# Experts' weights rotate through three places instead of two, and TensorE's expert loop runs over six experts

## The chip, the cores and the metric

The kernel runs on 1 core of one Trainium2 chip. The metric is device time in microseconds (us) from the start to the end of one launch; the median of three runs is compared. All data are float32.

## The reference

One layer of a decoder over 1024 tokens of width 1024. Three token mixers (RWKV-7, chunkwise mLSTM, sliding-window attention) are computed from one input projection, gated, merged and projected; then comes a mixture of experts, which is the part that the change touches:

```python
x = x + gt1 * hybrid_mixer(h, ...)
h = rms_norm(x, norm2_g) * (1 + sc2) + sh2
x = x + gt2 * hier_moe(h, w_rg, b_rg, w_re, b_re, w_e_in, w_e_out)

def expert_block(args):                      # 32 experts, each token goes to 2 of them
    xs, e = args                             # w_e_in[e] is 1024 x 1024, w_e_out[e] 512 x 1024
    gate, up = jnp.split(xs @ w_e_in[e], 2, axis=-1)
    return (jax.nn.silu(gate) * up) @ w_e_out[e]
```

## The kernel before

A router gives every token two of the 32 experts, and an indirect DMA sorts the tokens' rows into slots of 96 per expert (`x_slots` in DRAM). Then the 32 experts run one after the other, each with one block of up to 96 tokens. (Experts with more tokens get extra blocks behind the loop; with these inputs there are none, and that code is jumped over.)

One expert is 144 matmuls of the program on TensorE (PE). `first(s, w, j)` is one half of the product with `w_e_in` (48 matmuls for j = 0, 48 for j = 1), `second(w)` is the product with `w_e_out` (48). `step(e, ...)` waits for the weights and calls both halves of `first`; `close(e, ...)` waits for the weights of the output product and for the activations, and calls `second`. PE runs step(e), close(e - 1), step(e + 1), close(e), so that the activation of one expert (ScalarE: SiLU; VectorE: product, transposes) lies beside the next expert's first product. Each float32 matmul of the program is two LDWEIGHTS and two MATMULs in the trace: 288 MATMULs per expert.

An expert's weights are three pieces of 2048 KB: two halves of `w_e_in`, then `w_e_out`. A place in SBUF holds the three pieces of one expert. `WE` has two such places, at columns 0 and 12288 of the arena. A third set of tiles, `WX` at columns 24576 to 36863, holds expert 2 only, and is not filled again. Expert 3 goes to place 0, expert 4 to place 1, and from there on the two alternate: `next_in(e, s, used)` on SyncE (SP) waits until PE has used each half of the expert that was in place s and then issues the DMA of that half (line 468), `next_out` does this for `w_e_out` (line 472) after a wait on `y`, which counts two for each finished `second`. All of these go through SP's one DMA queue (q1) in the order written. The token rows of the experts are loaded (line 1700) and the results stored (lines 1731, 1732) through ScalarE's queue (q10).

PE's code for experts 0 to 3 is written out; experts 4 to 31 run in a loop over two experts (`pe.Fori(2, NE // 2)`, line 1351, 14 rounds). SP, ScalarE and VectorE have loops over two experts as well. In three gaps of its loop VectorE does the rest of the router's work (`blocks_counted`, `blocks_placed`, `blocks_owned`).

Behind the experts GpSimd gathers for every token its two results from `y_slots` (line 759), VectorE adds them to the rows `f_x` that SP has loaded from `x1` (line 540), and ScalarE stores the output. At the end of PE's loop, line 1360 is the branch that jumps over the code for extra blocks.

Of the kernel before, what the change touches and what calls it, by code (L numbers as in the profile page):

```python
# [5 lines left out]
T, D = 1024, 1024  # L6
P = 128
NT, KT = T // P, D // P
H, N = 4, 64
CH = 8  # L10
NG, NE, TOPK, DE = 4, 32, 2, 512
# [10 lines left out]
def hybrid_block(nc, I, out, dram):  # L22
# [6 lines left out]
    with ctx:  # L29
        SB = ctx.enter_context(nc.sbuf_tensor("arena", [P, 52992], f32))[:, :]  # L30
        PS = [ctx.enter_context(nc.psum_tensor(f"bank{i}", [P, 512], f32))[:, :] for i in range(8)]
        sems = {}

        def sem(name):
            if name not in sems:
                sems[name] = ctx.enter_context(nc.semaphore(name))
            return sems[name]

        def view(off, *dims):

            n = 1
            for d in dims:
                n *= d
            v = SB[:, off:off + n]
            if len(dims) == 2:
                v = v.rearrange("p (a b) -> p a b", a=dims[0])
            if len(dims) == 3:
                v = v.rearrange("p (a b c) -> p a b c", a=dims[0], b=dims[1])
            return v
# [7 lines left out]
        VECS, MOD1, WR_SHIFT, WR_SCALE, WR_BIAS = range(1, 6)  # L57
        COUNTS, EXTRAS, X_TABLE = range(NT + 1, NT + 4)
        IDENT, CONSTS, Q_TILE, _, _, _, R_IOTA, R_IOTAP = range(1, 9)
        COND, ADA_ROW, _, _, _, A_TANH, A_GSIG = range(1, 8)  # L60

        K_ACT, K_DVE = (1, 4, 7), (0, 2, 3, 5, 6)
# [113 lines left out]
        FW = view(0, 8, P)  # L176
        FWS = [FW, view(1024, 8, P)]
        s_fill = [sem("fill_w"), sem("fill_wb")]
        FWC = view(1024, 4, P)
        FWB, FBB = view(1536, 8, P), view(2560, 2, P)  # L180
# [97 lines left out]
        i_ix = [sb_i[:, 152:153], sb_i[:, 153:154], sb_i[:, 154:155]]  # L278

        WE = [[view(12288 * s + 4096 * j, 4, 1024) for j in range(3)] for s in range(2)]  # L280
        WX = [view(32768, 4, 1024), view(24576, 4, 1024), view(28672, 4, 1024)]
        e_xs = [view(TMP0 + 2322 + D * s, D) for s in range(2)]
        e_xT = [view(TMP0 + KT * CAP * s, KT, CAP) for s in range(2)]
        e_h, e_hT, e_g = view(36864, 3, P), view(37248, 4, CAP), view(37632, 3, P)
        e_hTl = view(38784, 4, CAP)
# [1 line left out]
        E_GU = [PS[3], PS[4], PS[7]]  # L287
        gt2, gt2b = view(TMP1 + 1056, 768), view(38912, 768)

        f_x = [view(12288 + 1024 * t, D) for t in range(NT)]  # L290
        f_y = [[view(2048 * i, D), view(2048 * i + 1024, D)] for i in range(4)]

        def bc(ap, n):
# [3 lines left out]
        def mm(o, l, r, start=True, stop=True):  # L297
            return nc.tensor.matmul(o, l, r, start=start, stop=stop)  # L298
# [23 lines left out]
        vec_rows, n = [], 0  # L322
# [21 lines left out]
        for r in range(4):  # L344
            slot_count[r % 2] += 16 * len(slot_loads(r))
            slot_target.append(slot_count[r % 2])
        s_slot = [sem("weights_slot0"), sem("weights_slot1")]

        fy_in = [(sem("fy_in0"), 0), (sem("fy_in1"), 0), (sem("x_sc0"), 16 * NT), (sem("x_sc1"), 16 * NT)]

        m_in = [(sem("wide_in0"), 80), (sem("wide_in1"), 80), (s_slot[0], slot_target[2]), (s_slot[1], slot_target[3])]
# [16 lines left out]
        def _(sp):  # L368
# [98 lines left out]
            def w_in_half(e, s, j):  # L467
                sp.dma_start(WE[s][j], I["w_e_in"][0, ds(e, 1), 512 * j:512 * j + 512, :]
                             .rearrange("a (p k) n -> p (a k) n", p=P)).then_inc(sem(f"win{s}{j}_in"), 16)

            def w_out_of(e, s):
                sp.dma_start(WE[s][2], I["w_e_out"][0, ds(e, 1)]
                             .rearrange("a (p k) n -> p (a k) n", p=P)).then_inc(sem(f"wout{s}_in"), 16)
# [25 lines left out]
            sp.wait_ge(sem("o_mm"), 12)  # L499
            w_out_of(1, 1)  # L500
            sp.wait_ge(sem("o_mm"), 16)
            def third(j):
                sp.dma_start(WX[j], I["w_e_in"][0, 2:3, 512 * j:512 * j + 512, :]
                             .rearrange("a (p k) n -> p (a k) n", p=P)).then_inc(sem("merge_w"), 16)

            third(0)
            sp.wait_ge(sem("xs0_in"), 16)
            third(1)
            sp.wait_ge(sem("x_used"), 2 * NT)
            for t in range(2):  # L510
                sp.wait_ge(sem(f"rows_st{t}"), 16 * NT // 2)
                sp.wait_ge(sem(f"xn_st{t}"), 16 * NT // 2)
                sp.wait_ge(sem(f"x_sc{t}"), 16 * NT)
            sp.dma_start(WX[2], I["w_e_out"][0, 2:3].rearrange("a (p k) n -> p (a k) n", p=P)).then_inc(sem("merge_w"), 16)

            def next_in(e, s, used):
                sp.wait_ge(sem("win_half"), used)
                w_in_half(e, s, 0)
                sp.wait_ge(sem("win_used"), used)
                w_in_half(e, s, 1)  # L520

            def next_out(e, s, used):
                sp.wait_ge(sem("y"), 2 * used)
                w_out_of(e, s)

            next_in(3, 0, 1)
            next_in(4, 1, 2)
            next_out(3, 0, 1)
            next_out(4, 1, 2)
            next_in(5, 0, 4)  # L530
            with sp.Fori(3, NE // 2) as i:
                next_in(2 * i, 1, 2 * i - 1)
                next_out(2 * i - 1, 0, 2 * i - 2)
                next_in(2 * i + 1, 0, 2 * i)
                next_out(2 * i, 1, 2 * i - 1)
            next_out(NE - 1, 0, NE - 2)

            sp.wait_ge(sem("win_used"), NE - 1)
            for t in range(NT):
                sp.dma_start(f_x[t], x1_t[t]).then_inc(sem("gate_in"), 16)  # L540

# [3 lines left out]
            with sp.If(n_extra > 0):  # L545
                with sp.Fori(0, NX) as j:
                    with sp.If(n_extra > j):
                        e = sp.value_load(i_ex[0:1, ds(j, 1)], min_val=0, max_val=NE - 1)
# [216 lines left out]
        def _(pe):  # L765
# [526 lines left out]
            def first(s, w, j):  # L1292
                for k in range(4):
                    w_k = w[j][:, k, :].rearrange("p (h q n) -> p h q n", h=2, q=4)
                    for r in range(3):
                        for c in range(4):
                            t, q = (c, r) if c < 3 else (r, 3)
                            ins = mm(E_GU[r][32 * c:32 * c + 32, 0:256].rearrange("p (h n) -> p h n", h=2),
                                     e_xT[s][:, 4 * j + k, ts(t, QT)], w_k[:, :, q, :],
                                     j == 0 and k == 0, j == 1 and k == 3)  # L1300
                return ins

            def second(w, hT=e_hT):
                for r in range(3):
                    for k in range(4):
                        for c in range(4):
                            t, q = (c, r) if c < 3 else (r, 3)
                            ins = mm(PS[5 + r // 2][32 * c:32 * c + 32, ts(r % 2, 256)], hT[:, k, ts(t, QT)],
                                     w[2][:, k, ts(q, 256)], k == 0, k == 3)
                    if r:  # L1310
                        ins.then_inc(sem("y"), 1)

            def step(e, s, w, turn):
                pe.wait_ge(sem(f"win{w}0_in"), 16 * turn + 16)
                pe.wait_ge(sem("e_xT"), e + 1)
                pe.wait_ge(sem("e_act"), e)
                first(s, WE[w], 0).then_inc(sem("win_half"), 1)
                pe.wait_ge(sem(f"win{w}1_in"), 16 * turn + 16)
                first(s, WE[w], 1).then_inc(sem("win_used"), 1)

            def close(e, w, turn, hT=e_hT):
                pe.wait_ge(sem("e_hT"), e + 1)
                pe.wait_ge(sem(f"wout{w}_in"), 16 * turn + 16)
                pe.wait_ge(sem("y_out"), 2 * e)
                second(WE[w], hT)

# [7 lines left out]
            first(0, WE[0], 1).then_inc(sem("win_used"), 1)  # L1334

            step(1, 1, 1, 0)
            pe.wait_ge(sem("e_hT"), 1)
            pe.wait_ge(sem("wout0_in"), 16)
            second(WE[0])

            pe.wait_ge(sem("merge_w"), 96)
            pe.wait_ge(sem("e_xT"), 3)
            pe.wait_ge(sem("e_act"), 2)
            first(0, WX, 0).then_inc(sem("win_half"), 1)
            first(0, WX, 1).then_inc(sem("win_used"), 1)
            close(1, 1, 0)
            step(3, 1, 0, 1)
            pe.wait_ge(sem("e_hT"), 3)
            pe.wait_ge(sem("y_out"), 4)
            second(WX)  # L1350
            with pe.Fori(2, NE // 2) as i:
                e = 2 * i
                step(e, 0, 1, i - 1)
                close(e - 1, 0, i - 1)
                step(e + 1, 1, 0, i)
                close(e, 1, i - 1)
            close(NE - 1, 0, NE // 2 - 1, e_hTl)
            pe.wait_ge(sem("router_dve"), EXTRAS)
            n_extra = pe.value_load(i_ex[0:1, NX:NX + 1], min_val=0, max_val=NX)
            with pe.If(n_extra > 0):  # L1360
# [1133 lines left out]
```

## Time and profile before

| | |
|---|---|
| median of 3 runs | 1783.63 us (1782.71 to 1785.6) |
| span of the profiled execution, first to last instruction | 1778.4 us |
| what the median has beyond that span | 5.2 us |
| PE busy | 1670.4 us, 94% of the span |
| expert stage on PE | about 1212 to 1736 us |
| behind the last matmul (store, gather, add, output) | 42.3 us |

A time in the profile counts from the span's start. PE, PEld (weight load), DVE (VectorE), ACT (ScalarE), POOL (GpSimd) and SP are engines; a q behind the name, as SPq or PEldq, is the engine's sequencer. PEclk is the clock that TensorE was granted, 1.00 for full speed (2.4 GHz) and 0.50 for half. "DMA share" is the mean busy share of the 16 DMA engines; it can come out a little over 1. In a list of waits or of a timeline, "[1.32 <-DVE ...]" says that the engine sat idle 1.32 us before this, and what ended it. Queue q8 carries PE's own instructions.

### The profile page before, as it was taken

What the parts mean: (1) busy time and instruction counts of PE and PEld (TensorE: products, weight loads), DVE (VectorE), ACT (ScalarE), POOL (GpSimd) and SP (SyncE); (2) the same over time, 40 slices, a digit from 0 to 9 for tenths busy, and PEclk for the clock granted to TensorE, in tenths of its full rate; (3) what the DMA queues carried; (4) which work ended last, traced back from release to release, by engine and by line L of the source; (5) the groups of instructions that cost most, each with busy time, mean ns of one, the idle gap of its engine ahead of it and who ended that gap; (6) DMA issues with size and microseconds to landing.
All of it is one profiled execution on the core that took longest, in us unless ns stands there. A gap on an engine that the chain in (4) does not pass through costs nothing.

```text
span 1778.4 us, 35422 instructions
## 1 busy us (share of the span) xinstructions
PE 1670.4 (94%) x14793; PEld 930.9 (52%) x14793; DVE 1012.6 (57%) x2453; ACT 442.4 (25%) x1072; POOL 211.8 (12%) x311
## 2 busy tenths in 40 slices
PE   5999999999999999999999999987999999999990
PEld 3455444544444545555455545545777775555550
DVE  2486526555555354443544435555778877776754
ACT  5120324333444212222122121112222122122110
POOL 3030000000110222202222051010000000000003
PEclk9999999999999999999999999988999999999995
DMA  9377218001211110101101176489899999999997
GB/s 350 120 265 252 71 71 263 25 24 32 63 48 52 47 33 16 33 21 31 34 16 33 56 292 232 148 284 370 330 425 427 426 427 426 429 427 427 429 422 303
DMA packets 109014, 363.70 MB, mean 205 GB/s; under 512 B 12890, under 2 KB 56840, under 8 KB 96428
## 3 DMA queue, kind: packets, MB, share of 16 engines
q1 hardware_dynamic: 86256, 282.70, 41.0%
q10 hardware_dynamic: 15708, 54.73, 8.4%
q0 software_dynamic: 6960, 25.04, 3.8%
q8 instruction: 60, 0.98, 0.2%
q14 instruction: 30, 0.25, 0.0%
HBM read 316.42 MB, written 58.74 MB: 211 GB/s over the span
## 4 chain that ended last, share of the span: by engine, by line
PE 80%; DMA 14%; DVE 3%; POOL 1%; issue 1%; ACT 1%; SPq 1%; ACTq 0%; POOLq 0%; DVEq 0%
PE bank L298 78%; DMA arena<-in_w_e_out 11%; DMA arena<-in_w_in 1%; POOL arena L759 1%; PE bank L945 1%; DMA arena<-y_slots,ints 1%; SPq L380 1%; DVE arena L2396 0%; DVE arena L1887 0%; PE bank L1233 0%; ACTq L1397 0%; DMA arena<-in_kn_g_c 0%; DVE arena L2386 0%; ACT arena L1523 0%; DMA x_slots<-arena,ints 0%
## 5 line engine op out<-in xcount | busy, mean ns | idle before, releaser
L298 PE MATMUL bank<-arena 128*32 128x256 f32 (+7 forms) x14414 | 1627.4, 388 | 36.4 <-DMA arena<-in_w_e_in 7.1
L298 PEld LDWEIGHTS bank<-arena 128*32 128x32 f32 (+3 forms) x14414 | 884.7, 131 | 748.5 <-issue 548.1
L2386 DVE STREAM_TRANSPOSE arena<-arena 32x256 f32<-32x256 f32 x372 | 161.9, 435 | 5.7
L2396 DVE STREAM_TRANSPOSE arena<-arena 32x128 f32<-32x128 f32 x384 | 157.5, 410 | 4.8
L1725 ACT ACTIVATE arena<-bank 128x128 f32<-128x128 f32 x96 | 19.7, 278 | 395.4 <-PE bank L298 395.4
L1717 ACT ACTIVATE arena<-arena 128x96 f32<-128x96 f32 x248 | 92.1, 460 | 5.2 <-DVE arena L2386 5.2
L2377 DVE TENSOR_TENSOR arena<-bank,arena 128x512 f32<-128x512 f32 x64 | 35.5, 557 | 99.9 <-PE bank L298 99.8
L2144 DVE TENSOR_TENSOR arena<-arena,bank 128x128 f32<-128x128 f32 (+1 forms) x40 | 11.4, 286 | 130.3 <-PE bank L298 130.3
L759 POOL DMA_INDIRECT arena<-y_slots,ints x16 | 17.1, 1070 | 542.9 <-DMA y_slots<-arena 537.9
L684 POOL TENSOR_TENSOR arena<-arena 64x256 f32<-64x256 f32 x96 | 70.2, 731 | 30.3 <-DVE arena L2120 23.7
L1887 DVE RECIPROCAL arena<-arena 128x512 f32<-128x512 f32 x10 | 33.5, 3349 | 30.8 <-ACT arena L1452 30.8
L1854 DVE SCALAR_TENSOR_TENSOR arena<-arena 128x512 f32<-128x512 f32 x56 | 42.1, 752 | 2.0
L1650 ACT ACTIVATE arena<-bank 128x128 f32<-128x128 f32 x40 | 11.1, 277 | 129.4 <-PE bank L298 129.4
L2114 DVE TENSOR_TENSOR arena<-arena,bank 128x512 f32<-128x512 f32 x32 | 21.9, 685 | 33.8 <-PE bank L298 33.3
L2368 DVE TENSOR_TENSOR arena<-arena,bank 128x128 f32<-128x128 f32 x96 | 21.8, 283 | 28.8 <-ACT arena L1725 28.1
L690 POOL TENSOR_TENSOR arena<-arena 128x512 f32<-128x512 f32 x8 | 10.2, 1270 | 232.4 <-DVE arena L2114 232.4
L1965 DVE SCALAR_TENSOR_TENSOR arena<-arena,bank 128x256 f32<-128x256 f32 x64 | 21.9, 414 | 23.8 <-PE bank L298 23.8
L1684 ACT ACTIVATE arena<-arena 128x1024 f32<-128x1024 f32 x8 | 8.5, 1057 | 104.9 <-DVE arena L2285 104.9
L1531 ACT ACTIVATE arena<-bank 128x512 f32<-128x512 f32 x16 | 9.6, 598 | 93.0 <-PE bank L298 93.0
L1523 ACT ACTIVATE arena<-arena 128x256 f32<-128x256 f32 x64 | 31.5, 493 | 0.0
L725 POOL DMA_INDIRECT x_slots<-arena,ints x16 | 15.7, 981 | 118.9 <-DVE ints L2266 94.0
L1630 ACT ACTIVATE arena<-bank 128x512 f32<-128x512 f32 x32 | 19.1, 596 | 34.7 <-PE bank L298 34.6
(337 smaller groups left out, 1030.1 us busy)
## 6 DMA issues: line engine op xcount, KB each, us to landing
arena<-in_w_e_in SPq DMA_DIRECT2D x64, 2048.0 KB, 24.4
arena<-in_w_e_out SPq DMA_DIRECT2D x32, 2048.0 KB, 25.2
arena<-in_w_ada SPq DMA_DIRECT2D x12, 2048.0 KB, 12.4
arena<-in_w_in SPq DMA_DIRECT2D x32, 512.0 KB, 3.8
arena<-x_slots ACTq DMA_DIRECT2D x32, 512.0 KB, 10.3
y_slots<-arena ACTq DMA_DIRECT2D x32, 288.0 KB, 9.3
y_slots<-arena POOLq DMA_DIRECT2D x21, 384.0 KB, 17.2
arena<-in_w_in SPq DMA_DIRECT2D x3, 2048.0 KB, 21.3
```

Of the source, the lines that this page charges most:

```text
L298: return nc.tensor.matmul(o, l, r, start=start, stop=stop)
L684: G.tensor_tensor(a_lo[q][b], a_sm[b, :, 0, b], lvl[b, q, b].unsqueeze(1).to_broadcast([N, H, N]), ALU.mult).then_inc(sem("a_lo"), 1)
L759: pool.indirect_dma_start(out=f_y[t % 4][k], out_offset=None, in_=yslot_d, in_offset=bass.IndirectOffsetOnAxis(ap=ix[:, t:t + 1], axis=0))\
L1523: ins = A.activation(c_sc[:, j, :], c_sc[:, j, :], ACT.Exp, bias=c_nm[:, j:j + 1], accum_out=c_sum[:, j:j + 1])
L1717: ins = A.activation(e_xT[s][:, k, :], e_xT[s][:, k, :], ACT.Identity, scale=sc2e[:, k:k + 1], bias=sh2e[:, k:k + 1])
L1854: ins = STT(acc, w[:, k, :], cond[:, k:k + 1], acc, ALU.mult, ALU.add)
L1887: link(V.reciprocal(c_rs[half], c_rs[half]))
L1965: ins = STT(c_sc[:, 2 * i + a, :], dist[:, 1 if c else 0, :], -slope, PS[2 + 2 * a + i // 2][:, ts(i % 2, 2 * P)], ALU.mult, ALU.add)
L2114: TT(dst, m_sg[n % 2], PS[7], ALU.mult).then_inc(sem("m_prod"), 1)
L2377: TT(e_y[s][:, cols], PS[5 + u][:, 0:(512, 256)[u]], gt2[:, cols], ALU.mult).then_inc(sem("y_out"), 1)
L2386: ins = V.transpose(e_xT[s][ts(b, QT), :, ts(t, QT)], rows[:, :, b, :])
L2396: ins = V.transpose(hT[ts(q, QT), :, ts(t, QT)], e_h[ts(c, QT), r, :].rearrange("p (n k) -> p k n", k=4))
```

## The change

`WX` becomes the third place of `WE`, and expert e goes to place e mod 3 all the way. SP refills each place when PE has used it, which is three experts back and no longer two. The semaphores of the third place are older ones that are used again, with the count they already have as an offset (`again`, `begun`). PE's code is written out for experts 0 to 7, and experts 8 to 31 run in a loop over six experts, 4 rounds: six, since the places repeat after three experts and the tiles for tokens after two. The rows `f_x` move to the third place's columns, and their load waits until expert 29 is closed, where it waited until the first product of expert 30 was done. The loops of VectorE and ScalarE are not touched.

```diff
+        again = {"win20_in": ("wide_in0", 96), "win21_in": ("wide_in1", 96), "wout2_in": ("part_st", 16 * NT)}
+
+        def begun(name):
+
+            return again[name][1] if name in again else 0
...
-        WX = [view(32768, 4, 1024), view(24576, 4, 1024), view(28672, 4, 1024)]
+        WE.append([view(32768, 4, 1024), view(24576, 4, 1024), view(28672, 4, 1024)])
...
-        f_x = [view(12288 + 1024 * t, D) for t in range(NT)]
+        f_x = [view(24576 + 1024 * t, D) for t in range(NT)]
...
             next_in(3, 0, 1)
             next_in(4, 1, 2)
             next_out(3, 0, 1)
+            next_in(5, 2, 3)
             next_out(4, 1, 2)
-            next_in(5, 0, 4)
-            with sp.Fori(3, NE // 2) as i:
-                next_in(2 * i, 1, 2 * i - 1)
-                next_out(2 * i - 1, 0, 2 * i - 2)
-                next_in(2 * i + 1, 0, 2 * i)
-                next_out(2 * i, 1, 2 * i - 1)
-            next_out(NE - 1, 0, NE - 2)
-
-            sp.wait_ge(sem("win_used"), NE - 1)
+            with sp.Fori(2, (NE - 2) // 3) as i:
+                next_in(3 * i, 0, 3 * i - 2)
+                next_out(3 * i - 1, 2, 3 * i - 3)
+                next_in(3 * i + 1, 1, 3 * i - 1)
+                next_out(3 * i, 0, 3 * i - 2)
+                next_in(3 * i + 2, 2, 3 * i)
+                next_out(3 * i + 1, 1, 3 * i - 1)
+            next_in(NE - 2, 0, NE - 4)
+            next_out(NE - 3, 2, NE - 5)
+            next_in(NE - 1, 1, NE - 3)
+            next_out(NE - 2, 0, NE - 4)
+            next_out(NE - 1, 1, NE - 3)
+
+            sp.wait_ge(sem("y"), 2 * (NE - 2))
...
             def step(e, s, w, turn):
-                pe.wait_ge(sem(f"win{w}0_in"), 16 * turn + 16)
+                pe.wait_ge(sem(f"win{w}0_in"), 16 * turn + 16 + begun(f"win{w}0_in"))
...
-            pe.wait_ge(sem("merge_w"), 96)
-            pe.wait_ge(sem("e_xT"), 3)
-            pe.wait_ge(sem("e_act"), 2)
-            first(0, WX, 0).then_inc(sem("win_half"), 1)
-            first(0, WX, 1).then_inc(sem("win_used"), 1)
+            step(2, 0, 2, 0)
             close(1, 1, 0)
-            step(3, 1, 0, 1)
-            pe.wait_ge(sem("e_hT"), 3)
-            pe.wait_ge(sem("y_out"), 4)
-            second(WX)
-            with pe.Fori(2, NE // 2) as i:
-                e = 2 * i
-                step(e, 0, 1, i - 1)
-                close(e - 1, 0, i - 1)
-                step(e + 1, 1, 0, i)
-                close(e, 1, i - 1)
-            close(NE - 1, 0, NE // 2 - 1, e_hTl)
+            for e in range(3, 8):
+                step(e, e % 2, e % 3, e // 3)
+                close(e - 1, (e - 1) % 3, (e - 1) // 3)
+            with pe.Fori(1, (NE - 2) // 6) as i:
+                for j in range(6):
+                    step(6 * i + j + 2, j % 2, (j + 2) % 3, 2 * i + (j + 2) // 3)
+                    close(6 * i + j + 1, (j + 1) % 3, 2 * i + (j + 1) // 3)
+            close(NE - 1, (NE - 1) % 3, (NE - 1) // 3, e_hTl)
```

On PE, the written-out experts and the loop before, in the order of the program (the matmuls in a run are counted together; the loop lies between the two branches of line 1351):

```order
L298 MATMUL bank<-arena 32x256 x528
L1351 UNCONDITIONAL_BRANCH
...
L298 MATMUL bank<-arena 32x256 x96
L1324 ISA
L298 MATMUL bank<-arena 32x256 x48
L1314 ISA
L1315 REGISTER_ALU
L298 MATMUL bank<-arena 32x256 x96
L1324 REGISTER_ALU
L298 MATMUL bank<-arena 32x256 x48
L1351 REGISTER_ALU
L1351 COMPARE_AND_BRANCH
```

The same now, with the first two and the last two of the loop's six experts (the lines have moved: L305 is the old L298, L1355 the loop):

```order
L305 MATMUL bank<-arena 32x256 x1104
L1355 UNCONDITIONAL_BRANCH
...
L305 MATMUL bank<-arena 32x256 x96
L1333 REGISTER_ALU
L305 MATMUL bank<-arena 32x256 x48
...
L305 MATMUL bank<-arena 32x256 x96
L1333 REGISTER_ALU
L305 MATMUL bank<-arena 32x256 x48
L1355 REGISTER_ALU
L1355 COMPARE_AND_BRANCH
```

The written-out part has grown from 528 to 1104 matmuls of the program, and the loop's body from 2 times 144 = 288 to 6 times 144 = 864.

On SP, the refills behind the first three experts up to the loop, before (line 468 loads a half of `w_e_in`, line 472 loads `w_e_out`):

```order
L468 DMA arena<-in_w_e_in 128x4096 x4
L472 DMA arena<-in_w_e_out 128x4096 x2
L468 DMA arena<-in_w_e_in 128x4096 x2
L531 UNCONDITIONAL_BRANCH
L531 ISA
```

And now (lines 475 and 479):

```order
L475 DMA arena<-in_w_e_in 128x4096 x4
L479 DMA arena<-in_w_e_out 128x4096
L475 DMA arena<-in_w_e_in 128x4096 x2
L479 DMA arena<-in_w_e_out 128x4096
L534 UNCONDITIONAL_BRANCH
```

Expert 5's two halves now stand ahead of expert 4's `w_e_out`, and wait for expert 2 where they waited for expert 3.

## Rows read from the trace of the kernel before

**Rows 1.** Busy time by stretch: us, busy and count by engine, PEclk, DMA share, GB/s
```profile
1240.00:1280.00 40.00, 40.00 (x748) 29.19 (x744) 31.38 (x77) 6.96 (x22) 0.00 (x0) 1.00 0.84 324
1280.00:1290.00 10.00, 10.00 (x192) 7.28 (x185) 6.50 (x18) 3.48 (x11) 0.00 (x0) 1.00 0.98 397
1290.00:1725.00 435.00, 422.12 (x7712) 276.40 (x7708) 324.47 (x830) 90.79 (x289) 0.00 (x0) 1.00 1.01 427
```
**Rows 2.** Chain that ended last, expert stage: start us, us, what
```profile
1205.39 3.33 DMA arena<-x_slots
...
1225.44 140.10 PE bank L298 x2592
...
1661.92 27.94 DMA arena<-in_w_e_out
1689.86 0.23 issue
1690.10 31.33 PE bank L298 x576
```
**Rows 3.** Timeline: start us, us, engine, line, what, count, idle before
```profile
1241.23 15.87 SPq L472 DMA_DIRECT2D arena<-in_w_e_out  x2
1261.95 21.20 SPq L468 DMA_DIRECT2D arena<-in_w_e_in  x4
...
1382.36 17.91 PE L298 MATMUL bank<-arena 128*32 128x256 f32 x328 [1.32 <-DVE arena L2368]
...
1600.08 5.39 PE L298 MATMUL bank<-arena 128*32 128x256 f32 x96 [0.56 <-DMA arena<-in_w_e_in]
...
1711.47 7.05 SPq L540 DMA_DIRECT2D arena<-x  x8
...
1729.06 7.07 PE L298 MATMUL bank<-arena 128*32 128x256 f32 x96 [2.50 <-DVE arena L2377]
...
1747.20 1.28 DVE L2470 SCALAR_TENSOR_TENSOR arena<-arena 128x1024 f32<-128x1024 f32 x1 [10.59 <-DMA arena<-y_slots,ints]
```
**Rows 4.** Lines 1351 and 1360 on PE's sequencer: ns min/median/max, first and last start
```profile
L1351 PEldq COMPARE_BRANCH  x14: 76/208/248, 1302.0 to 1725.2; - x14
...
L1360 PEldq COMPARE_BRANCH  x1: 3654/3654/3654, 1735.6 to 1735.6; - x1
```
**Rows 5.** DMA queues of the whole span: packets, MB, share of 16 engines
```profile
q8 instruction: 60, 0.98, 0.2%
```
**Rows 6.** Stretch 1208 to 1302: its busy times, then its DMA queue q8
```profile
1208.00:1302.00 94.00, 89.97 (x1620) 64.21 (x1624) 65.61 (x163) 23.63 (x71) 0.00 (x0) 0.96 0.93 371
...
q8 instruction: 13, 0.21, 0.8%
```
**Rows 7.** Stretch 1330 to 1730: all its DMA queues, and the issues of x_slots
```profile
q1 hardware_dynamic: 10801, 149.62, 87.7%
q10 hardware_dynamic: 8619, 21.04, 13.3%
q14 instruction: 3, 0.02, 0.0%
...
arena<-x_slots ACTq DMA_DIRECT2D x22, 512.0 KB, 10.3
```
**Rows 8.** Busy time by stretch around PE's last pause
```profile
1726.00:1729.00 3.00, 0.56 (x12) 0.08 (x4) 2.83 (x7) 0.00 (x0) 0.00 (x0) 1.00 1.02 408
1729.00:1730.00 1.00, 0.94 (x20) 0.73 (x24) 0.00 (x0) 0.00 (x0) 0.00 (x0) 1.00 1.04 414
1730.00:1734.00 4.00, 4.00 (x49) 2.58 (x45) 0.00 (x0) 0.00 (x0) 0.00 (x0) 0.57 1.02 406
```

More of the change, by code:

```diff
@@ L32, in hybrid_block @@
         sems = {}
+        again = {"win20_in": ("wide_in0", 96), "win21_in": ("wide_in1", 96), "wout2_in": ("part_st", 16 * NT)}
+        def begun(name):
+            return again[name][1] if name in again else 0
         def sem(name):
+            name = again.get(name, (name,))[0]
             if name not in sems:
@@ L501, in _ @@
             sp.wait_ge(sem("o_mm"), 16)
[L502 to L506, printed above, removed]
+            w_in_half(2, 2, 0)
             sp.wait_ge(sem("xs0_in"), 16)
-            third(1)
+            w_in_half(2, 2, 1)
             sp.wait_ge(sem("x_used"), 2 * NT)
@@ L513, in _ @@
                 sp.wait_ge(sem(f"x_sc{t}"), 16 * NT)
-            sp.dma_start(WX[2], I["w_e_out"][0, 2:3].rearrange("a (p k) n -> p (a k) n", p=P)).then_inc(sem("merge_w"), 16)
+            w_out_of(2, 2)
             def next_in(e, s, used):
@@ L1317, in step @@
                 first(s, WE[w], 0).then_inc(sem("win_half"), 1)
-                pe.wait_ge(sem(f"win{w}1_in"), 16 * turn + 16)
+                pe.wait_ge(sem(f"win{w}1_in"), 16 * turn + 16 + begun(f"win{w}1_in"))
                 first(s, WE[w], 1).then_inc(sem("win_used"), 1)
@@ L1322, in close @@
                 pe.wait_ge(sem("e_hT"), e + 1)
-                pe.wait_ge(sem(f"wout{w}_in"), 16 * turn + 16)
+                pe.wait_ge(sem(f"wout{w}_in"), 16 * turn + 16 + begun(f"wout{w}_in"))
                 pe.wait_ge(sem("y_out"), 2 * e)
```

## The prediction, made before the changed kernel was run

> **What bounds the kernel now.** I read the busy times by stretch first, since an average over the whole span hides the expert stage. There the reader is to see two engines at their limits [rows 1]. From 1290 to 1725 us the DMA engines are full (share 1.01, 427 GB/s), while PE is busy 422 of 435 us. Before that, from 1240 to 1280, PE is full and the DMA engines are not: share 0.84, 324 GB/s. The chain of waits says the same in its own way [rows 2]: from 1225.44 on PE alone for 140.10 us, later PE and the landings of `w_e_out` in turn, 27.94 us from issue to landing, and at the very end PE alone again.
>
> One expert costs PE 288 matmuls of the trace at 140.10 / 2592 = 54.05 ns, 15.57 us. It costs the DMA engines three pieces of 2048 KB, a load of tokens of 512 KB and a store of 384 KB, 7.21 MB in all, or 16.9 us at 427 GB/s. So weights arrive 1.3 us per expert too slowly, and what counts is how early the queue is filled and whether it ever runs dry. It ran dry between expert 3's `w_e_out` at 1241.23 and expert 5's first half at 1261.95 [rows 3]: nothing but expert 4's `w_e_out` could be asked for, as both places were full.
>
> **Two floors under the last matmul.** It ends at 1729.06 + 7.07 = 1736.13 us [rows 3]. Behind it lie 42.3 us of gathering and output up to 1778.4; I take that part as unchanged, since it hangs on the last expert's store alone.
>
> *DMA floor.* With the third place expert 5's halves stand ahead of expert 4's `w_e_out` and wait for expert 2, some 15.6 us earlier, so the hole closes. What it is worth: 40 us times (427 - 324) plus 10 us times (427 - 397) is 4.42 MB [rows 1], at 427 GB/s 10.3 us. Against that stands the code that PE has to fetch in addition (below): 59 packets of 16 KB, 0.97 MB, 2.3 us. The DMA floor is 1736.1 - 10.3 + 2.3 = 1728.1 us.
>
> *PE floor.* With weights always there PE runs from 1225.44 at 54.05 ns. Of the stage's 9216 matmuls 192 lie before that, so 9024 remain: 487.7 us, to 1713.2. Three things stay: 1.3 us for VectorE's `blocks_counted` at 1382.36, 2.5 us before the last product, which waits for the last activations, and 1.7 us because that product took 7.07 us where others take 5.39 [rows 3]. Together 1718.7 us, 17.4 before the present end. The other two pieces of router work on VectorE show no stall now, and their cover (PE's next first product) stays.
>
> So without anything new on PE the DMA floor would decide, and the kernel would win 8 us.
>
> **What the longer loop adds.** Queue q8 carries 60 packets for 0.98 MB, 16 KB each [rows 5]. From 1208 to 1302 PE began 1620 MATMULs and 1624 LDWEIGHTS and took 13 packets [rows 6]: a packet is about 250 instructions, and PE was running straight ahead. From 1330 to 1730 there are 170 MB in q1 and q10 and not one packet in q8 [rows 7]. In that time the loop over two experts went round; its 288 times 4 = 1152 instructions are 4.6 packets, and they stayed in the engine's store. The branch back takes 208 ns there [rows 4]. The one branch that jumps to code which had not been fetched, at 1735.6 over the extra blocks (about 670 instructions, 2.7 packets ahead), takes 3654 ns [rows 4]. I could not have seen that in the list of busy engines, since it sits on PE's sequencer.
>
> The loop over six experts is 864 times 4 = 3456 instructions, 13.8 packets, three times what the trace shows to stay. Whether it stays is not in this trace: the bounds are 0 (all of it stays) and 3654 - 208 = 3446 ns and more at each return (nothing of the loop's head is left). I take the second, the case nearer to the only long jump that was measured. There are 4 rounds, so 3 returns. The packets: 576 more matmuls of the program written out and 576 more in the loop's body, times 4, over 250, are 18; three rounds fetched again at 13.8 are 41; 59 together.
>
> The Trainium skill ("Runtime: NRT & Kernel Launch", section "Instruction fetch mechanics") has PE's instruction memory as 128 KiB, 2048 instructions, filled in blocks of 16 KiB. By that a body of 1152 stays and one of 3456 does not, which is the case I took; the trace agrees in the size of the packet and in the small loop. The same section says that a taken branch whose target is outside a window of two blocks stalls for a fetch. Here the trace disagrees: returns over 4.6 blocks took 208 ns and fetched nothing. By that rule the old loop would already have paid 13 times 3.4 us, the new one 3 times, and the change would win about 34 us; with those two rows against it I give that no chance.
>
> What one return costs:
> - the branch: 3.45 us.
> - the wait of its packet behind the weights. The 3654 ns were measured with the DMA engines half idle. A load of `x_slots` lands after 3.33 us on nearly free engines [rows 2] and after 10.3 us on full ones [rows 7], 7.0 us more for the 8 packets that it has on each engine. One packet lies between 7.0 / 8 = 0.9 and 7.0 us; I take 2.5, nearer the low end, since it is one packet and no eight in a row.
> - the clock. PE paused 2.50 us before its last product [rows 3], and then, from 1730 to 1734, the granted clock was 0.57, so mostly 1.2 GHz [rows 8]; the 5.39 us product took 7.07. A pause of 1.32 us at 1382.36 did no such thing (clock 1.00 over 1290 to 1725) [rows 1]. A pause of 6 us should cost at least that: 1.7 us.
>
> Together 7.6 us, three times 22.9. PE is then on its own floor: 1718.7 + 22.9 = 1741.6 us, later than the DMA floor's 1728.1. That matters: in the old kernel PE had 1.3 us per expert to spare, and a stall of 6 us would have been absorbed within five experts. Now that the weights come early, nothing absorbs it.
>
> **Edits that I cost at nothing.** Expert 2's step no longer waits for its `w_e_out`: PE ran through there without a gap. The rows `f_x` waited for expert 30's first product and now wait for expert 29's close; but in the old queue they stood behind expert 31's `w_e_out`, which waits for that same close, and they were issued at 1711.47 [rows 3]. They are first used at 1747.20, and have about 24 us of cover. The extra register instructions of PE's loop are hidden, as those of the old one.
>
> **Rivals.**
> 1. *The loop stays in the store.* Then nothing is fetched again, only 18 packets more once (0.7 us), and the DMA floor decides: 1736.1 - 10.3 + 0.7 = 1726.5, 9.6 us faster: 1774.0 us. For it: the small loop did stay, and nothing in the trace shows a limit. Against it: 13.8 packets is a lot. Chance 0.15.
> 2. *The returns are cheap.* Only the 3.45 us each, if the packet passes the weights and the clock holds: 1718.7 + 10.3 = 1729.0, 7.1 us faster, 1776.5 us; chance 0.10. With the clock's 1.7 us, but no wait behind weights: 1734.1, 2.0 faster, 1781.6 us; chance 0.15. For it: straight code at full DMA load shows no gap, so packets do come through.
> 3. *Each return waits for two packets.* The loop's head need not lie at the start of a packet; if little of the first one is left, PE waits at once for the second: 3 x (2 x (3.45 + 2.5) + 1.7) = 40.8 us, last matmul at 1759.5, 1807 us at the worst, and about 1798 if half of the second wait is covered. It decides as soon as less than some 6 us of work is left in the first packet, which holds about 7. Slower than before by 14 to 23 us. Chance 0.10, as the head's place in its packet is not known and the fetch may run ahead meanwhile.
> 4. *Forecast:* 7.6 us each, between 6 and 9.5. Chance 0.50.
>
> **How the numbers follow.** The forecast's last matmul is 5.5 us later than now, so the span is 1783.9 us and with the 5.2 us beyond it 1789.1; I say 1789. Its own range is 1784 to 1795. A measurement of this kernel tells about 0.2%, 3.6 us, from no change. Faster than 1780.1: rival 1 and the first half of rival 2, 0.25. Within: the second half of rival 2 and the forecast's low end, 0.20. Slower than 1787.2: the rest of the forecast and rival 3, 0.55. The range reaches down over rival 2 and to rival 1's time, and up to where rival 3 begins: 1773.5 to 1796.
>
> **What would show it.** The loop's COMPARE_BRANCH on PE's sequencer should stand there 4 times, three of them at 5 us or more; q8 should carry about 120 packets, 40 of them during the loop; PE should have three pauses of about 6 us, after experts 12, 18 and 24 are closed, each with a dip of the clock behind it, and hardly any wait for weights; and the share of 0.84 from 1240 to 1280 should be gone. If q8 stays near 78 and the long branches are missing, rival 1 holds. If the pauses are there and PE still waits for weights as well, my DMA floor is too low.

## The result, and the profile after

| | before | after |
|---|---|---|
| median, 7 runs each | 1783.14 us | 1789.99 us (1789.03 to 1790.97) |
| span of the profiled execution | 1778.4 us | 1788.4 us |
| expert stage on PE, second expert's first matmul to the last | 1225.44 to 1736.13, 510.7 us | 1230.30 to 1745.96, 515.7 us |
| packets of PE's code (q8) | 60 | 123 |

The changed kernel is 0.37% slower: 1.0037 times the time before, with a 95% interval of 1.0026 to 1.0048.

The two profiled executions differ by 10.0 us, the medians by 6.9. The expert stage accounts for 5.0 us of it. Another 4.9 us lie ahead of the stage, where no instruction was changed. In the profiles of all kernels run later the second expert starts between 1229.0 and 1234.8 us, also where PE's code up to there is that of the kernel before (1230.7 and 1229.7). So the profiled execution of before, with 1225.44, was a quick one up to there. About 2 of the 6.9 us stay unexplained.

Busy time by stretch, after (the columns are those of [rows 1]):

```profile
1240.00:1280.00 40.00, 40.00 (x749) 29.20 (x744) 28.54 (x71) 10.41 (x33) 0.00 (x0) 1.00 1.01 416
1290.00:1400.00 110.00, 108.69 (x2020) 79.00 (x2014) 87.15 (x220) 24.04 (x77) 0.00 (x0) 1.00 1.01 424
1400.00:1500.00 100.00, 94.40 (x1720) 58.30 (x1716) 73.70 (x191) 20.19 (x65) 0.00 (x0) 0.97 1.01 424
```

The hole in the weights' stream is closed: a share of 1.01 from 1240 to 1280 us, where [rows 1] had 0.84. Behind 1400 us PE's clock is 0.97 on average; from 1290 to 1725 us it was 1.00 [rows 1].

PE's timeline in the expert stage, after (start, us, what, count, idle before and what ended it):

```profile
1230.30 155.61 PE L305 MATMUL bank<-arena 128*32 128x256 f32 x2880 [1.54 <-DVE arena L2370]
1387.22 46.83 PE L305 MATMUL bank<-arena 128*32 128x256 f32 x864 [1.31 <-DVE arena L2370]
1439.65 95.07 PE L305 MATMUL bank<-arena 128*32 128x256 f32 x1728 [5.60 <-issue]
1540.13 96.02 PE L305 MATMUL bank<-arena 128*32 128x256 f32 x1728 [5.41 <-issue]
1641.69 94.75 PE L305 MATMUL bank<-arena 128*32 128x256 f32 x1728 [5.54 <-issue]
1738.89 7.07 PE L305 MATMUL bank<-arena 128*32 128x256 f32 x96 [2.46 <-DVE arena L2379]
```

Three pauses of 5.4 to 5.6 us, one behind each round of 1728 MATMULs, and "issue" as their end: PE waited for nothing that another engine or a transfer releases. There is no wait for weights left. Who ended PE's waits, then total us, times, longest, for the longest entry:

```profile
PE bank L305 <- issue: 16.5, 3, 5.6
```

From the second expert on PE's only other waits are for VectorE, 5.4 us in all. Behind each pause 1728 MATMULs run without a second wait, so rival 3 did not happen here. The clock dips behind each pause: 1728 MATMULs at 54.05 ns are 93.4 us, and the rounds took 95.07, 96.02 and 94.75. Around the first pause, busy time by stretch:

```profile
1434.00:1440.00 6.00, 0.40 (x7) 0.21 (x8) 5.71 (x15) 0.00 (x0) 0.00 (x0) 0.68 1.02 426
1440.00:1447.00 7.00, 7.00 (x108) 3.69 (x104) 4.57 (x11) 0.00 (x0) 0.00 (x0) 0.79 1.01 424
1447.00:1460.00 13.00, 13.00 (x248) 7.34 (x244) 4.20 (x12) 3.45 (x11) 0.00 (x0) 1.00 1.00 421
```

The branches on PE's sequencer, after, which answer to [rows 4] (ns min/median/max):

```profile
L1355 PEldq COMPARE_BRANCH  x4: 83/6400/6557, 1432.7 to 1735.1; - x4
...
L1362 PEldq COMPARE_BRANCH  x1: 3805/3805/3805, 1745.3 to 1745.3; - x1
```

The queue that carries PE's code, after, over the whole span (packets, MB, share), which answers to [rows 5]:

```profile
q8 instruction: 123, 2.02, 0.5%
```

### The profile page after: what moved, and what is told of

It reads as the page before. It is cut to its first block, busy times and chain, and to the rows that moved or that the text cites. A ratio compares the mean times of both kernels' runs of the same rounds, so it can differ in the third digit from the quotient of the medians.

```text
span 1788.4 us, 35353 instructions
## 1 busy us (share of the span) xinstructions
PE 1675.2 (94%) x14793; PEld 916.3 (51%) x14793; DVE 1011.4 (57%) x2453; ACT 442.4 (25%) x1072; POOL 211.9 (12%) x311
## 4 chain that ended last, share of the span: by engine, by line
PE 90%; DVE 3%; DMA 3%; issue 2%; POOL 1%; ACT 1%; SPq 1%; ACTq 0%; POOLq 0%; DVEq 0%
PE bank L305 88%; DMA arena<-in_w_in 1%; POOL arena L768 1%; PE bank L954 1%; DMA arena<-y_slots,ints 1%; SPq L387 1%; DVE arena L2398 0%; DVE arena L1889 0%; PE bank L1242 0%; DMA arena<-in_kn_g_c 0%; ACTq L1399 0%; DVE arena L2388 0%; ACT arena L1525 0%; DMA x_slots<-arena,ints 0%; DMA arena<-x_slots 0%
## 5 line engine op out<-in xcount | busy, mean ns | idle before, releaser
L305 PE MATMUL bank<-arena 128*32 128x256 f32 (+7 forms) x14414 | 1632.2, 391 | 41.9 <-issue 20.2
L305 PEld LDWEIGHTS bank<-arena 128*32 128x32 f32 (+3 forms) x14414 | 869.8, 132 | 773.6 <-issue 559.5
## 6 DMA issues: line engine op xcount, KB each, us to landing
y_slots<-arena ACTq DMA_DIRECT2D x32, 288.0 KB, 10.8
```

## The experiments

Three theories were at hand. T: the third place wins what was worked out, and three far returns of PE's loop (returns to code that has left the store) cost more. A: the third place itself, or the deeper queue, is slow. B: two places never cost anything. All kernels were timed against the kernel before.

**No return: PE's experts written out.**

```diff
-            for e in range(3, 8):
+            for e in range(3, NE):
                 step(e, e % 2, e % 3, e // 3)
                 close(e - 1, (e - 1) % 3, (e - 1) // 3)
-            with pe.Fori(1, (NE - 2) // 6) as i:
...
```

> Three places, PE's experts 3 to 31 written out, so no return at all. Theory (three returns of 7.4 us each cost what the third place wins): PE has no long branch, its floor is 17 us under the old end, and the DMA floor decides, 10.3 us less 2.3 us for 60 more packets of code: about 1775 us, 8 us faster than before, PE waits for weights again, share of the DMA engines 1.01 all through. Rival A (the third place itself or the deeper queue is slow): near 1790 us, as with the loop. Rival B (two places never cost anything): near 1783 us.

Measured: 1787.5 us, ratio 1.0018 (1.0007 to 1.0029). No long branch and weights waited for again, as T said, but 12.5 us slower than T's number. It is 2.5 us faster than the changed kernel, with intervals that just overlap, so this run alone says little about the returns, and it excludes neither A nor B. Something costs here that T does not have.

**One return: a loop over twelve.**

```diff
-            with pe.Fori(1, (NE - 2) // 6) as i:
-                for j in range(6):
+            with pe.Fori(0, 2) as i:
+                for j in range(12):
...
```

> Three places, loop over twelve experts, two rounds, so one return in place of three. Theory: PE's floor plus one return, 1718.7 + 7.4 = 1726.1, lies under the DMA floor of 1728.1, so the return is hidden and the time is that of the kernel without returns, about 1775 us. Rival (every return is on the path): 7.4 us above the kernel without returns, about 1782 us. Rival A (third place is slow): near 1790 us.

Measured: 1786.51 us, ratio 1.0017 (1.0008 to 1.0026), with one branch of 6.1 us. That is the time of the kernel without returns (the intervals cover each other): one return hides behind the weights, as forecast. The level is again too high, by 11.5 us.

**Four returns: everything from expert 2 on in the loop over six.**

```diff
-            step(2, 0, 2, 0)
-            close(1, 1, 0)
-            for e in range(3, 8):
...
-            with pe.Fori(1, (NE - 2) // 6) as i:
+            with pe.Fori(0, (NE - 2) // 6) as i:
```

> Three places, experts 2 to 31 all in the loop over six, five rounds and four returns in place of three. Theory: PE is on its floor, one more return adds its full 7.4 us: 1790.0 + 7.4 = 1797.4 us, four branches of 6.4 us and one of under 0.1 us, four pauses of 5.5 us. Rival A (the loop is not what costs): 1790 us.

Measured: 1801.2 us, ratio 1.0099 (1.0084 to 1.0115), 11 us above the changed kernel. Each return is on the path, and A's number of 1790 us falls: the places are the same. The 11 us are more than one return of 7.4 us, because all four cost more here. In the profile they cost 34.0 us, 8.5 each: 22.3 us of pauses, and 11.7 us in the MATMULs behind them, against 54.05 ns each. Behind the first pause of each return come 47 MATMULs and then a second, short pause of 0.3 to 0.7 us, as in rival 3 but much smaller.

**Two places with the long loop.**

```diff
-            with pe.Fori(2, NE // 2) as i:
+            for i in range(2, 4):
...
+            with pe.Fori(1, (NE - 2) // 6) as r:
+                for j in range(3):
+                    e = 6 * r + 2 + 2 * j
+                    step(e, 0, 1, 3 * r + j)
...
```

> Two places as before, but PE's code as in the changed kernel: written out to expert 7, then a loop over six, three returns. Theory: the weights arrive 1.3 us per expert slower than PE works, so PE gets each return's 7.4 us back within six experts; only the code's packets cost, 2.3 us: 1784 to 1786 us, with three branches of 6.4 us on the sequencer. Rival (a return costs its full time wherever it stands): 1783 + 22 = 1805 us.

Measured: 1795.75 us, ratio 1.0067 (1.0053 to 1.0081), between the two numbers, so not decided by itself. The next run has the same places and as much code, but no return.

**Two places, PE written out: the old kernel without any return.**

```diff
-            with pe.Fori(2, NE // 2) as i:
+            for i in range(2, NE // 2):
                 e = 2 * i
```

> Two places as before, PE's experts written out, so that the thirteen short returns are gone. Theory: a return within the store costs 0.2 us on the sequencer and nothing on PE, and 26 more experts' code is 60 packets, 0.98 MB, 2.3 us of the DMA engines, which are the bound: 1783 to 1786 us. Rival (short returns cost too, by the rule of a window of two blocks): up to 40 us faster than before, bounded by the weights: near 1775 us.

Measured: 1796.68 us, ratio 1.0072 (1.0059 to 1.0086). Both numbers missed. That short returns cost PE nothing is better seen in the kernel before: it ran from 1225.44 us on for 140.10 us without a gap, across a return at 1302.0 [rows 2, rows 4]. So what this run adds is 59 packets of code (119 against 60), and it costs 12.8 us (0.72% of 1783) where I had 2.3. And with about the same amount of code (123 and 119 packets) three far returns more or less make no difference: with two places PE gets them back. In the kernel above PE waited 4.7 us for weights beside its three pauses of 16.0 us. B falls: with PE written out in both, two places are 9.2 us slower than three. PE's waits in the expert stage of this kernel (who ended the wait, then total us, times, longest):

```profile
PE bank L298 <- DMA arena<-in_w_e_in: 13.6, 16, 2.3
...
PE bank L298 <- issue: 6.2, 13, 1.8
```

The kernel before waited 7.1 us for `w_e_in` and 4.4 for `w_e_out`, 13 times each. The 13 waits that end with "issue" all stand ahead of `close`, where the kernel before waited for `w_e_out`, so I take them for waits for `w_e_out`; that a part of them is PE waiting for its own code is not excluded. The weights did come later: their last piece landed 500.9 us behind the second expert's first matmul before, and 512.8 us here, 11.8 of the 12.1 us by which the stage grew.

So code costs by delaying weights, and over five times more than its bytes. The trace shows a reason where SP's queue ends, with the last weights and the rows `f_x`. From 1700 to 1760 us, 40 slices of 1.5 us, tenths of the DMA engines' busy time. First before:

```profile
DMA  9999999999999998999999941710699989999999
GB/s 426 423 388 442 453 395 448 415 448 426 411 434 412 468 418 363 413 399 415 412 401 410 353 173 55 228 45 0 153 350 322 273 284 391 363 377 423 418 418 421
```

Then the kernel with three places and PE written out:

```profile
DMA  9999999999999898999999955477547420079997
GB/s 428 426 426 426 448 415 394 425 444 449 408 423 427 382 328 306 409 427 418 416 410 431 399 213 199 199 265 290 211 195 223 135 81 16 0 183 303 328 281 259
```

Before, the engines go idle within two slices. With the long code they work on for about eight slices (1735 to 1747) at half, some 200 GB/s. The last `w_e_out`, from issue to landing, before and then here:

```profile
arena<-in_w_e_out SPq DMA_DIRECT2D x1, 2048.0 KB, 15.3
arena<-in_w_e_out SPq DMA_DIRECT2D x1, 2048.0 KB, 30.9
```

The trace also records, for each piece of weights, 16 completions, one for each DMA engine. Before, the 16 lie within 3.5 us of each other through the whole stage. In the kernel with two places and PE written out they split into eight and eight: the gap between the eighth and the ninth is 0.7 us for the piece that landed at 1328.7, 1.8 us at 1514.7, 4.9 us at 1607.5 and 7.8 us at 1721.9. With three places and PE written out it is 10.0 us for the last piece. So eight engines fall steadily behind, and PE can start only when the last engine has brought its share. PE's code is what was added, 59 packets; if it is carried by 8 of the 16 engines, each has 7.4 more, at about 1.06 us with weights beside it, 7.8 us in all, near the gaps that are seen. That PE's code goes to these eight engines is inferred from this agreement; the trace does not name the engine of a packet, and no run placed the code elsewhere.

**Small refills.**

```diff
+            def bit_in(e, s, j):
+                sp.dma_start(WE[s][j][:, 0:1, 0:128], ...).then_inc(sem(f"win{s}{j}_in"), 16)
...
             def next_in(e, s, used):
                 sp.wait_ge(sem("win_half"), used)
-                w_in_half(e, s, 0)
+                bit_in(e, s, 0)
...
```

The other half of `w_e_in` and `w_e_out` are cut down in the same way. The kernel's output is wrong by this; it serves for its times only.

> The changed kernel, but from expert 3 on each refill brings 64 KB in place of 2048 KB (the experts' products then use old weights; all instructions of PE stay). It sizes the terms of one return. Theory: 2.7 us of the 6.4 us branch is its packet's wait behind the weights, so the three branches take 3.7 to 3.9 us, PE pauses 2.8 to 3.6 us at each, the clock still dips for 3.4 us behind each, 1.7 us. PE end is its floor plus 3 x 5.2, about 5 us earlier than in the changed kernel: about 1783 us. Rival (the distance of the jump sets its time, not the traffic): branches stay at 6.4 us, 1790 us.

Measured: 1778.05 us, ratio 0.9959 (0.9944 to 0.9975), 5 us under my number. The branches on PE's sequencer in this kernel, and then its rounds in PE's timeline:

```profile
L1360 PEldq COMPARE_BRANCH  x4: 82/3570/3720, 1436.5 to 1726.5; - x4
```

```profile
1440.56 93.45 PE L305 MATMUL bank<-arena 128*32 128x256 f32 x1728 [2.73 <-issue]
1536.74 95.13 PE L305 MATMUL bank<-arena 128*32 128x256 f32 x1728 [2.73 <-issue]
1634.32 93.45 PE L305 MATMUL bank<-arena 128*32 128x256 f32 x1728 [2.44 <-issue]
```

The long branches fall from 6.4 to 3.6 us: 2.8 us of each were its packet's wait behind weights. And after pauses of 2.4 to 2.7 us the clock dips once in three times (95.13), where it dipped each time behind 5.5 us. A return here costs 3.2 us on average where I had 5.2: 1.1 us less by the clock, as I had counted a dip for each, and 0.9 us less by the pause.

**A loop over three experts.** The tokens' tile `e_xT` gets a third place, so that everything on PE repeats after three experts; the loops of ScalarE and VectorE are written out for it. Body: 1744 instructions, 6.8 packets, 9 rounds.

```diff
+        e_xT.append(lvl.rearrange("p a b -> p (a b)")[:, 0:KT * CAP].rearrange("p (k n) -> p k n", k=KT))
...
+            START = 4
+            for e in range(2, START):
+                one(e)
+            with pe.Fori(1, 1 + (NE - START) // 3) as i:
+                for e in range(START - 3, START):
+                    step(3 * i + e, e % 3, e % 3, i + e // 3)
+                    close(3 * i + e - 1, (e - 1) % 3, i + (e - 1) // 3)
```

> Three places with a loop over three experts: the tokens get a third tile too, so that both repeat after three experts (ScalarE's and VectorE's experts are written out for it). PE's body is 1744 instructions, 6.8 packets, and by my count of instructions its head lies near the start of a packet; 9 rounds. Theory after the runs so far (weights come 10 us earlier by the third place; what eats it is code: 7.4 us for each far return, and about 0.2 us of the weights' landing for each packet, 60 packets being 12 us): if the body stays in the store, no long branch, q8 near 60 to 65 packets, and about 10 us faster than before, 1774 us. Rival (the store holds less than 7 or 8 packets): 8 branches of 6 us, q8 near 120, PE at its floor plus 8 x 7.4 us, near 1826 us.

Measured: 1780.77 us, ratio 0.9983 (0.9974 to 0.9993). The same kernel was timed again, beside the last kernel of this section:

> e7 again, for a comparison with e9 on one chip: 1779 to 1782 us, 0.1 to 0.25% faster than before.

Measured: 1779.53 us, ratio 0.9979 (0.9969 to 0.9988). The body stays: 9 short branches, 64 packets. It beats both kernels, by 0.2% and 0.6%, but not by the 10 us I gave it. Again there is a straggler, here a single engine: the last piece of weights was complete on fifteen engines within 4.2 us in the first run and 3.7 in the second, and on the sixteenth after 10.8 and 8.1. I did not find what it had carried. Besides PE's packets the kernel has 7 more in queue q14 (37 against 30), of about 0.3 us each. Set beside the kernel with PE written out (1787.5 us, 119 packets), 55 packets less are worth 7 us with three places. The branches on PE's sequencer in this kernel (ns min/median/max):

```profile
L1358 PEldq COMPARE_BRANCH  x9: 76/208/240, 1323.4 to 1712.1; - x9
```

**The same, with the head elsewhere.**

```diff
-            START = 4
+            START = 5
```

> The same with one more expert written out ahead of the loop, so that the body's 6.8 packets begin about 100 instructions into a packet and touch 8 of them in place of 7; 9 rounds. If the store has room for it, as e7: 1774 us. If the store holds 8 packets and one of them is always the next one ahead, the head is lost at each return: 8 long branches, near 1826 us, even if e7 has none.

Measured: 1829.74 us, ratio 1.0265 (1.0243 to 1.0287). The same branches in this kernel, and then two rounds of PE's timeline:

```profile
L1358 PEldq COMPARE_BRANCH  x9: 83/6307/6710, 1336.8 to 1771.8; - x9
```

```profile
1343.39 48.63 PE L306 MATMUL bank<-arena 128*32 128x256 f32 x864 [5.20 <-issue]
1397.48 48.68 PE L306 MATMUL bank<-arena 128*32 128x256 f32 x864 [5.46 <-issue]
```

One expert more ahead of the same loop, and all 8 returns are long: 49 us. The body has the same length; what differs is how many packets it touches, by my count 8 in place of 7. The queue agrees: q8 carries 136 packets where it had 64, 9 more for each return, so with one that is fetched ahead all 8 come again.

**More written out ahead of the loop.**

```diff
-            START = 4
+            START = 12
```

> As e7, but eight more experts are written out ahead of the loop: 6 rounds from expert 12 on. Eight experts move the head by 8 x 578 instructions, which is 18 packets and 16 instructions, so by my count it still lies near the start of a packet: no long branch, and 18 more packets of code, 82 on q8. Theory (a packet of code delays the weights by 0.1 to 0.2 us, since only some of the DMA engines carry code and the others wait for them at each landing): 2 to 4 us above e7. Rival (only far returns cost, the volume of code does not): the time of e7 within 1 us. If the head is off by more than I count: 5 long branches, near 1805 us.

Measured: 1780.93 us, ratio 0.9996 (0.9979 to 1.0012), against 0.9979 for the kernel with START = 4 beside it. No long branch, 85 packets. The medians are 1.4 us apart, the ratios 3 us, and the intervals overlap: it does not tell 2 us from none. So 21 packets cost 0 to 3 us, 55 cost 7 us with three places, and 59 cost 12.8 us with two.

## Why the prediction was right, and where it was not

- *The third place's gain, 10.3 us.* Right in place: the share of 0.84 became 1.01. In size it is near with PE written out in both, 1796.68 against 1787.5 us, 9.2 us. With a loop that stays in the store in both it was only 3 to 4 us (ratios 0.9983 and 0.9979). The engine that lags in that kernel may have taken the rest; no run shows it.
- *PE's floor.* Right. From 1230.30 us it gives 487.7 + 1.3 + 2.5 + 1.7 = 493.2 us without returns. The stage took 515.7, so the three returns cost 22.5 us, 7.5 each, where I had 22.9 and 7.6.
- *The return's terms.* The pause was 5.5 us (5.95 forecast), of which the wait behind weights is 2.8 of the branch's 6.4 us (2.5 forecast). The clock cost (95.07 + 96.02 + 94.75) - 3 x 93.4 = 5.6 us, 1.9 each (1.7 forecast). The 1.7 came from a pause of 2.5 us, and such a pause lowers the clock only sometimes, as the runs above show; a pause of 5 us always did.
- *The body leaves the store.* Right: three long branches, and 63 packets more in q8 (123 against 60) where I had 59. The limit of the store, open in the prediction, lies between a body that touches 7 packets and one that touches 8. The Trainium skill ("Runtime: NRT & Kernel Launch", section "Instruction fetch mechanics") gives 128 KiB in blocks of 16 KiB, so 8 blocks. The two runs agree with that if one block holds the code ahead, which no run shows by itself. Its window of two blocks for a branch does not: a return over 6.8 packets took 208 ns.
- *The DMA floor, 1728.1 us.* Wrong, in the term of the added code: 2.3 us for 59 packets by their bytes alone, where 59 packets measured 12.8 with two places. With that it reads 1736.1 - 10.3 + 12.8 = 1738.6. The forecast survived because PE's floor with its returns, 1741.6, still lay above it, as PE's missing waits for weights show. The stage of the kernel with three places and PE written out, 509.9 us, would put it at 1735.4. So the margin was 3 to 6 us, where I had 13.5: that it sufficed was luck. By the same error rival 1 would have been too good: a loop of that size that stayed would not be at 1774 us for sure, as the loop over three with 64 packets came to 1780.
- *"A stall of 6 us would have been absorbed in the old kernel."* Shown for two places: 1795.75 with three far returns, 1796.68 with none.
- *What a span lacks.* I put 5.2 us beyond the span to every kernel. The changed kernel has 1.8 (1790.2 against a span of 1788.4); the rest fits the quick start of the profiled execution of before. The stage grew by 5.0 us, where I had 5.5, and the median by 6.9. That the forecast of 1789 lies within 1 us of the median is therefore in part luck.

## What to carry to other kernels

Ask of every edit that lengthens a loop whether its body still fits in the engine's instruction store, where the loop's head lies in it, and what covers the return if not; the sign of a miss is a branch of microseconds on the sequencer and idle time that ended with "issue". A bottleneck that is removed takes with it the slack that hid such stalls. And where transfers bound the time, unrolled code is not free, as its packets run through the same DMA engines.

## What the runs showed of the hardware

- A branch to code that is not in PE's store took 3.4 to 3.8 us on quiet DMA engines and 6.0 to 6.7 us on full ones; one to code that is there took 0.21 us, over 4.6 and over 6.8 packets alike.
- A loop body of 1744 instructions of PE stayed in the store at one position and was lost at every return at another, one expert further on: 1780.8 and 1829.7 us.
- 59 more packets of PE's code, 0.97 MB, made a kernel with a stream of weights at 427 GB/s 12.8 us slower; eight of the 16 DMA engines fell behind the other eight, by 7.8 us near the end of the stream.
- PE's granted clock fell to 1.2 GHz behind each pause of 5.0 to 5.6 us, and behind one of three pauses of 2.4 to 2.7 us. In the twelve profiles the last product follows a pause of 2.2 to 2.5 us; it took 7.0 to 7.1 us in six of them and 5.39 us in the other six.
